# The final RMSNorm of a decoder block: sums of squares on TensorE, a factor of 128x4 numbers, and a final product shared by VectorE and GpSimd

## What is computed

```python
def rmsnorm(x, g):
    xf = x.astype(jnp.float32)
    y = xf * lax.rsqrt(jnp.mean(xf * xf, axis=-1, keepdims=True) + NORM_EPS)
    return (y * g.astype(jnp.float32)).astype(x.dtype)
...
        x = x + peer_ffn(h, peer_wq[l], peer_keys[l], peer_u[l], peer_v[l])
    return rmsnorm(x, norm_f_g)
```

## Time and profile before

| | us |
|---|---|
| median of 3 runs | 2179.66 |
| lowest and highest | 2178.71, 2181.95 |
| the profiled execution, its own time | 2179.81 |
| its span in the profile | 2178.0 |
| PE busy, share of the span | 2098.9 (96%) |
| DVE busy | 1365.6 (63%) |
| ACT busy | 841.6 (39%) |
| POOL busy | 375.0 (17%) |

### The profile page before, as it was taken

How to read it: one execution, slowest core, us unless ns; L and a number is a source line. 1 busy time by engine, 2 the same in 40 slices (tenths; PEclk the granted TensorE clock), 3 DMA queues, 4 the chain that set the end, 5 groups by cost and what they waited for, 6 DMA issues and landing times.

```text
span 2178.0 us, 37167 instructions
## 1 busy us (share of the span) xinstructions
PE 2098.9 (96%) x12954; PEld 1748.2 (80%) x12954; DVE 1365.6 (63%) x2822; ACT 841.6 (39%) x1194; POOL 375.0 (17%) x463
## 2 busy tenths in 40 slices
PE   5999999997999989999989999999999999999997
PEld 3878888885878868888868888888888888888885
DVE  5478666657999956677645555555555555555555
ACT  4555343423222236666643333333333333333332
POOL 0000000100035449999910000000000000000000
PEclk9999999998999989999999999999999999999998
DMA  4211211532234444555573443454444444454431
GB/s 150 83 50 51 72 48 60 184 119 74 69 120 145 142 144 184 202 199 201 202 237 124 151 159 124 151 159 125 149 159 124 150 159 127 147 159 127 147 101 39
DMA packets 156780, 289.45 MB, mean 133 GB/s; under 512 B 10496, under 2 KB 76160, under 8 KB 154144
## 3 DMA queue, kind: packets, MB, share of 16 engines
q1 hardware_dynamic: 153856, 276.86, 38.4%
q0 software_dynamic: 2848, 11.54, 1.4%
HBM read 231.73 MB, written 56.62 MB: 132 GB/s over the span
## 4 chain that ended last, share of the span: by engine, by line
PE 72%; issue 6%; DVE 1%; DMA 1%; POOL 0%; ACT 0%; DVEq 0%; POOLq 0%; SPq 0%; ACTq 0%
PE unit L350 72%; DMA gl<-g_dram 0%; POOL uL L2005 0%; DMA g_dram<-ge 0%; DVE x L1969 0%; DMA sgw<-gate_dram 0%; DVE rs L1966 0%; PE unit L791 0%; DVE rs L1410 0%; DVE x L1914 0%; DVE aL L1904 0%; DVE af L1899 0%; ACT L957 0%; ACT aH L957 0%; DVE wL L1401 0%
## 5 line engine op out<-in xcount | busy, mean ns | idle before, releaser
L350 PE MATMUL unit<-h2H,uH 128*128 128x512 f32 x1024 | 411.9, 402 | 2.9 <-POOL uL L2005 2.9
L350 PE MATMUL unit<-aH,vH 128*128 128x512 f32 x1024 | 399.3, 390 | 9.9 <-DVE vL L1908 9.9
L350 PE MATMUL unit<-h2H,uL 128*128 128x512 f32 x1024 | 400.2, 391 | 0.0
L350 PE MATMUL unit<-h2L,uH 128*128 128x512 f32 x1024 | 399.1, 390 | 0.0
L350 PE MATMUL unit<-aH,vL 128*128 128x512 f32 x1024 | 399.1, 390 | 0.0
L350 PE MATMUL unit<-aL,vH 128*128 128x512 f32 x1024 | 399.1, 390 | 0.0
L1908 DVE TENSOR_TENSOR vL<-vraw,vH 128x512 fp32r<-128x512 f32 x256 | 176.1, 689 | 235.7 <-ACT vH L957 235.7
L957 ACT ACTIVATE vH<-vraw 128x512 fp32r<-128x512 f32 x256 | 161.1, 630 | 414.5 <-PE unit L350 414.5
L2024 POOL TENSOR_SCALAR oh<-cst,e2s 128x128 f32<-128x128 f32 x384 | 266.0, 711 | 18.2 <-PE unit L350 13.3
L350 PEld LDWEIGHTS unit<-aH,vH 128*128 128x128 f32 x1024 | 192.7, 188 | 50.5 <-DVE vL L1908 10.3
L350 PEld LDWEIGHTS unit<-h2H,uL 128*128 128x128 f32 x1024 | 192.4, 188 | 41.6
(11 more groups left out here) (274 smaller groups left out, 2887.7 us busy)
## 6 DMA issues: line engine op xcount, KB each, us to landing
uraw<-uT SPq DMA_DIRECT2D x128, 512.0 KB, 4.2
vraw<-v_tab SPq DMA_DIRECT2D x256, 256.0 KB, 2.8
wraw<-wall SPq DMA_DIRECT2D x68, 512.0 KB, 3.5
w_dram<-wst SPq DMA_DIRECT2D x16, 2048.0 KB, 6.6
wg<-w_dram SPq DMA_DIRECT2D x32, 1024.0 KB, 6.5
g_dram<-ge SPq DMA_DIRECT2D x64, 256.0 KB, 2.2
gl<-g_dram SPq DMA_DIRECT2D x32, 512.0 KB, 7.5
gate_dram<-gst POOLq DMA_DIRECT2D x16, 256.0 KB, 2.5
```

What stands on the lines that cost most here:

```text
L350: return pe.matmul(out, lhsT, rhs, start=start, stop=stop, skip_group_check=True)
```

## The change

Five things change, all in the final norm:

1. The squares get a tile for each chunk (`sq3` with eight chunks), so ScalarE's waits for VectorE go. VectorE's eight additions (`grow_sum(2, ...)`) go.
2. TensorE makes the sums instead, token-major, as `conv_square` does: for each of the 8 chunks and each of the 4 tiles of 128 tokens one matmul with the squares as weights and one column of 1/1024 as the moving operand, 32 matmuls into 128x4 numbers of bank 7.
3. Root and reciprocal are taken of 128x4 numbers. The table of the root is loaded ahead of the squares, by a root of one constant column.
4. TensorE lays the factor out over 128x512, once into bank 6 (`rs3a`) and once into bank 7 (`rs3b`), 4 matmuls each. VectorE reads `rs3a` in PSUM. ScalarE copies `rs3b` to SBUF, into `rs3`, for GpSimd.
5. VectorE multiplies chunks 2 to 7 only. ScalarE multiplies chunks 0 and 1 by their gain between its squares, and GpSimd multiplies them by the factor. The stores go in the order 2, 3, 4, 0, 5, 6, 1, 7.

```diff
-            mean_square("ms3", 7, rs3, 2)
+            o = begin("ms3", 7)
+            for c in range(DC):
+                pe.wait_ge(sq_ready, 2 * DC + c + 1)
+                for t in range(TT):
+                    last = mm(o[:, t:t + 1], sq3[:, c, tile(t)], C(C_M1024)[:, 0:1], c == 0 and t == 0,
+                              c == DC - 1 and t == TT - 1)
+            last.then_inc(fill_sem("ms3"), 1)
+            for name, b in (("rs3a", 6), ("rs3b", 7)):
+                o = begin(name, b)
+                pe.wait_ge(rdev3_ready, 1)
+                for t in range(TT):
+                    last = mm(o[:, tile(t)], rdev3[:, 1, t:t + 1].broadcast_to([P, P]), C(C_ID))
+                last.then_inc(fill_sem(name), 1)
@@
-            for c in range(DC):
-                sp.wait_ge(y_ready, c + 1)
-                sp.dma_start(yT[c], x1[:, c, :]).then_inc(y_stored[c % 2], 16)
+            by_pool = 0
+            for k, c in enumerate((2, 3, 4, 0, 5, 6, 1, 7)):
+                if c < 2:
+                    by_pool += 1
+                    sp.wait_ge(y_pool_ready, by_pool)
+                else:
+                    sp.wait_ge(y_ready, c - 1)
+                sp.dma_start(yT[c], x1[:, c, :]).then_inc(y_stored[k % 2], 16)
@@
+            fn(rdev3[:, 0, 0:1], vc("eps", 0), ACT.Sqrt)
             for c in range(DC):
 
                 act.wait_ge(acc_added, 4 + 8 * (NG - 1) + (4 if c < 4 else c + 1))
-                if c >= 2:
-                    act.wait_ge(sum_grown, 2 * DC + c - 1)
-                fn(sq3[:, c % 2, :], x1[:, c, :], ACT.Square).then_inc(sq_ready, 1)
+                fn(sq3[:, c, :], x1[:, c, :], ACT.Square).then_inc(sq_ready, 1)
+                if c == 3:
+                    for k in range(2):
+                        act.wait_ge(sq_ready, 2 * DC + k + 1)
+                        fn(x1[:, k, :], x1[:, k, :], ACT.Copy, scale=vc("gf", k)).then_inc(y_scaled, 1)
             wait_filled(act, "ms3")
-            root(rs3[:, :], "ms3", 0).then_inc(take_sem("ms3"), 1)
+            fn(rdev3[:, 0, :], ps("ms3")[:, 0:TT], ACT.Sqrt, bias=vc("eps", 0)).then_inc(take_sem("ms3"), 1)
+            wait_filled(act, "rs3b")
+            fn(rs3[:, :], ps("rs3b")[:, :], ACT.Copy).then_inc(take_sem("rs3b"), 1)
@@
-                if not more:
-                    for c in range(4):
-                        grow_sum(2, rs3, sq3, c)
@@
-            for c in range(4, DC):
-                grow_sum(2, rs3, sq3, c)
             wait_taken(dve, "ms3")
-            tick(dve.reciprocal(rs3[:, :], rs3[:, :]))
-            after()
-            for c in range(DC):
-                stt(x1[:, c, :], x1[:, c, :], vc("gf", c), rs3[:, :], ALU.mult, ALU.mult).then_inc(y_ready, 1)
+            dve.reciprocal(rdev3[:, 1, :], rdev3[:, 0, :]).then_inc(rdev3_ready, 1)
+            wait_filled(dve, "rs3a")
+            for c in range(2, DC):
+                stt(x1[:, c, :], x1[:, c, :], vc("gf", c), ps("rs3a")[:, :], ALU.mult, ALU.mult).then_inc(y_ready, 1)
@@
+            pool.wait_ge(y_scaled, 2)
+            wait_taken(pool, "rs3b")
+            for k in range(2):
+                pool.tensor_tensor(x1[:, k, :], x1[:, k, :], rs3[:, :], ALU.mult).then_inc(y_pool_ready, 1)
```

More of the change, by code:

```diff
@@ L205, in build @@
     aL = at("aL", 141, [P, 2 * G, T], F32R)
-    sq3 = at("sq3", 16, [P, 2, T])
-    rs3 = at("rs3", 20, [P, T])
+    sq3 = at("sq3", 12, [P, DC, T])
+    rs3 = at("rs3", 28, [P, T])
+    rdev3 = at("rdev3", 30, [P, 2, TT])
     def C(i):
@@ L295, in build @@
             "vh_ready", "vl_ready", "unit_done", "sweep_done", "acc_added"])
-        y_ready, y_stored = sem("y_ready"), [sem(f"y{i}_stored") for i in range(2)]
+        rdev3_ready, y_scaled = sem("rdev3_ready"), sem("y_scaled")
+        y_ready, y_pool_ready = sem("y_ready"), sem("y_pool_ready")
+        y_stored = [sem(f"y{i}_stored") for i in range(2)]
         block = ctx.enter_context(nc.Block())
```

## The result

The changed kernel takes 2184.43 us in the median of 21 runs (2181.43 to 2186.96), the kernel before 2179.95 in 21 runs (2177.01 to 2182.20). The ratio is 1.002, with a 95% interval of 1.0013 to 1.0026: 4.5 us slower, just above the 4.4 us that the prediction took as the least that could be told from no change. The forecast was 3.4 us slower, to 2183.0.

The account below looks back on a forecast made before the run. TensorE's expert layer, 72% of the chain, bounds the kernel; the change touches only the 18.3 us tail. Later sums and layout, products and stores move the span from 2178.0 to 2181.4; 2179.66 plus 3.4 gives 2183.0, range 2178.5 to 2186.0.

Parts of the forecast that it names:

- the main term: Final norm: 64 narrow passes queue behind TensorE's last wide pass, at 0.1125 then 0.213; first product 3.0 us later.
- the fall of the clock: During the narrow sums: clock halves at 2163.7, sums there at 2170.0; a fall at 2162.5 gives 2171.1, at 2165.0 2168.8.
- the stretch from the first product to the end: Products and stores: first product at 2172.9, five stores left from 2176.6 behind GpSimd's chunk 0, end at 2181.4.
- Costs set at nothing: ScalarE's table load, one-column root and two scalings, together 2.8 us, fit in its 5.82 us idle before the fifth square.
- The split of the products: Final products: taking two from VectorE for GpSimd gains nothing, since the transfers take what it frees.
- Rival A: Narrow sums: passes stay fast, sums at 2167.1; total 2178.3 or 2180.1, no change that can be told; chance 0.18.
- Rival B: Final products: VectorE holds GpSimd off, its two end at 2178.4 and 2179.7; plus 5.2 us, 2184.9; chance 0.15.

Follow-up runs that it names:

- e4: Changed kernel with the 64 narrow passes made twice: sums took 24.0 us for 128 passes, tail 35.4 us against 22.8.
- e5: Changed kernel with one wide 128x512 matmul behind each of the 32 narrow ones: sums 14.4 us, tail 24.3 us against 22.8.
- e1: Changed kernel with VectorE adding the squares again, 8 narrow passes in place of 64: median 2179.08 us, ratio to before 0.9998.
- e2: Changed kernel with all eight products on VectorE, no second layout, stores 0 to 7: first product to end 8.1 us against 9.0, tail 21.8.
- e3: Changed kernel with stores in the order 2, 3, 4, 5, 6, 0, 7, 1: first product to end 8.1 us against 9.0, tail 21.0.
- e7: Changed kernel, float32, all products on VectorE, which also adds squares 0 to 3 and 6, 7; 32 narrow passes: 2176.36 us, ratio to before 0.9984.
- e8: Changed kernel, all products on VectorE, which adds squares 0 to 3; fp32r sums in 20 passes: median 2174.04 us, ratio to before 0.9972.

## Why the prediction was right

**The cause.** All three steps of the main term held. The passes started at time 0 and nothing held them up; their price was 0.1125 and then 0.213, as the convolution's norm had it; and narrow passes let the clock fall (e4, e5). e1 took the passes away and the loss with them.

**The size** came out a little low: 3.4 us forecast, 4.5 measured, inside the stated range. (Of the 1.4 us between 2183.0 and 2184.43, 0.3 is the kernel before, at 2179.95 in 21 runs and 2179.66 in the three that the sum started from.) Two terms were mis-sized. First, the fall of the clock: the sum took it at 2163.7, 4.0 us after time 0, the middle between two rows. In all nine profiled executions of this study without wide matmuls in between it fell at 2.25 to 3.79 after time 0, on average 3.2: none as late as the sum had it. Each us costs 0.89 (0.213/0.1125 less 1), so 0.7 us on average; in the changed kernel's profile, with the fall at 2.8, the sums were done 0.8 us later than forecast. The late row came from a stretch with 32 matmuls of 64x64 between the last wide pass and the narrow ones:

```profile
372.17 1.43 PE L350 MATMUL unit<-r_in,state 64*64 64x64 f32 x32
```

The tail has none of them, and the row of the tail itself was the nearer one, although TensorE is idle there. In e1 it is idle too, and the clock fell at 3.8, ahead of e1's narrow passes. So the seven executions with narrow passes from time 0 (2.25 to 3.79) kept the clock about as long as the two without (2.7 and 3.8). With a fall at 2162.5 the text had plus 4.5. Second, the stretch from the first product to the end: 8.5 forecast, 9.0 measured. GpSimd's two products took 2.49 together (2.6 assumed), and chunk 0 was ready 3.7 us after the first product, as forecast; but the transfers after the pause began 0.8 behind their issue and the span ended 0.8 behind the last of them, where the sum had 0.7 each. Both were 0.8 in the kernel before already: the first slice with transfers in the earlier trace rows is half empty, so they begin at about 2171.56 and not at 2171.4. The terms also add up to 2181.5, not 2181.4, and the five transfers took 3.6 for 3.5. In the other direction the first product came 2.2 behind the end of the reciprocal, where the sum had 2.4.

**Costs set at nothing** were nothing: ScalarE's scalings ended at 2157.1, long before its fifth square, and the last square was ready 1.6 us after time 0, before TensorE reached chunk 4.

**The split of the products** gains nothing: e2 and e3 show 8.1 with and without GpSimd. The text had it so for the transfers' sake. It saw that stores stand behind chunk 0, but its sum has 0.4 of the 0.9 us that this costs, and it didn't ask for an order without that wait.

**Rival A** (fast passes) is refuted by the windows of the changed kernel and by e4. The formula of the Trainium skill ("TensorE: Matmul & The Clock Gate", section on LDWEIGHTS) gives 107 ns for a weight load of 128 columns. The pitch agrees at the higher clock (0.1125) and not at the lower, where it is 0.213 here as in the earlier trace rows (7.5 us for about 35 passes).

**Rival B** (GpSimd held off by VectorE) is refuted: the two products took 2.49 from 2178.55 on, while VectorE's ran until 2180.13. The Trainium skill ("GPSIMD Engine Reference", Specifications) names two SBUF inputs or a two-port mode as the cause of contention; with its factor in PSUM VectorE's product reads one tensor in SBUF (and one gain for each partition), and the trace agrees.

## What to carry to other kernels

Read on which engine's queue a moved sum ends up, and behind what: work that was free beside a busy engine cost the full price behind it. Count narrow matmuls by passes: here each, with new weights of 128x128, took 0.11 or 0.21 us for one moving column or two. (PEld was busy all through them, so the weights are the likely price; no run varied them.) Reduce first with an idle engine, then go to the narrow form (e7, e8), and keep the small root and reciprocal: with them e1's first product comes 1.6 us before that of the kernel before. Where the last stage is bound by its stores, a second engine for the arithmetic gave nothing, and a store order that waits for the slower engine cost 0.9.

## What was not expected

- TensorE that was busy without a gap ran at half clock for 20 us (e4), with passes one column wide. The clock rose while the 128-column passes of the layouts ran there, but not in the changed kernel.
- The time at which the clock falls, and with it about 1.4 us of the changed kernel's sums, differs between executions: 2.25 to 3.79 us after time 0. A term that depends on it needs a range, and e8 shows the way round it: be done before.
- In e7's profiled execution one store's issue took 0.90 us in place of 0.34 to 0.46, with nothing in the view of the waits that it waited for.
